# Expert stage of a transformer layer: gather and weight load of one block queued side by side, five blocks ahead

## The reference, cut to what matters

```python
# channel mixing: hierarchical MoE
h = modulate(rmsnorm(x, norm2_g[l]), sh2, sc2)
x = x + g2 * hierarchical_moe(h, ...)
return rmsnorm(x, final_g)

def hierarchical_moe(h, ...):      # 2048 tokens of 1024 per core, 32 experts, 2 per token
    ...                            # top-1 group of 4, then top-2 experts of its 8; combine = gates
    for e in range(N_EXPERTS):
        a, u = jnp.split(t @ w_up[e], 2, axis=-1)             # 1024 -> 2 x 256
        y = y + combine[:, e:e + 1] * ((jax.nn.silu(a) * u) @ w_down[e])
```

## Time and profile before

| | us |
|---|---|
| median of three runs | 1277.55 (1265.26 to 1277.86) |
| the profiled execution | 1271.89 |
| its span, slowest core (core 0) | 1270.2; the eight cores 1251.4 to 1270.2 |
| mean granted TensorE clock, core 0 | 0.811 |
| TensorE busy | 905.8 (71%) |
| VectorE busy | 584.3 (46%) |
| ScalarE busy | 411.5 (32%) |
| GpSimd busy | 333.0 (26%) |

### The profile page before, as it was taken

How to read it: one execution, slowest core, us unless ns; L and a number is a source line. 1 busy time by engine, 2 the same in 40 slices (tenths; PEclk the granted TensorE clock), 3 DMA queues, 4 the chain that set the end, 5 groups by cost and what they waited for, 6 DMA issues and landing times. The chain is left out here.

```text
span 1270.2 us, 17508 instructions; the slowest of 8 cores (1251.4 to 1270.2 us)
## 1 busy us (share of the span) xinstructions
PE 905.8 (71%) x6394; PEld 546.5 (43%) x6394; DVE 584.3 (46%) x1000; ACT 411.5 (32%) x833; POOL 333.0 (26%) x347
## 2 busy tenths in 40 slices
PE   1436999977899999789933357687688788787500
PEld 0134644444544444444422226465465565565300
DVE  1258527341247274424646863333334333343398
ACT  0046321255522212682232202233233333232332
POOL 3100000135300001460000013455456455464200
PEclk9755999975599999889975558788789888898855
DMA  8974154599627434612995106957767668764284
GB/s 173 169 167 131 25 77 66 64 154 151 157 66 108 71 63 69 99 31 104 140 171 144 59 6 133 186 124 148 145 131 140 152 133 177 159 120 104 97 283 173
DMA packets 75010, 154.64 MB, mean 122 GB/s; under 512 B 16930, under 2 KB 53282, under 8 KB 70448
## 3 DMA queue, kind: packets, MB, share of 16 engines
q0 software_dynamic: 61248, 111.28, 50.9%
q1 hardware_dynamic: 13680, 42.25, 9.8%
HBM read 287.20 MB, written 37.22 MB: 255 GB/s over the span
## 5 line engine op out<-in xcount | busy, mean ns | idle before, releaser
L279 PE MATMUL ps<-s_HT,s_ER 128*128 128x512 bf16 (+1 forms) x1232 | 257.0, 358 | 10.1 <-DMA s_ER<-win 4.0
L279 PEld LDWEIGHTS ps<-s_HT,s_ER 128*128 128x128 bf16 x1232 | 111.6, 98 | 142.0 <-issue 15.4
L1085 ACT ACTIVATE s_OV<-ps 128x512 bf16<-128x512 f32 x188 | 101.5, 601 | 143.7 <-PE ps L279 143.5
L1069 DVE TENSOR_TENSOR s_MT<-ps,s_MT 128x256 bf16<-128x256 f32 x94 | 39.9, 425 | 226.1 <-ACT s_MT L1068 151.5
L1039 POOL DMA_INDIRECT s_XG<-hd,s_toki x94 | 105.1, 1119 | 145.3 <-DVE s_MT L998 116.9
L279 PE MATMUL ps<-s_ER,s_MT 128*128 128x512 bf16 x464 | 120.1, 419 | 0.5 <-DVE s_ER L1074 0.5
L1052 PE MATMUL ps<-s_identb,s_XG 128*128 128x128 bf16 x752 | 63.1, 249 | 74.0 <-DMA s_XG<-hd,s_toki 74.0
L1092 POOL DMA_INDIRECT yd<-s_OV,s_rowi x94 | 95.0, 1011 | 61.1 <-ACT s_OV L1085 27.6
L279 PE MATMUL ps<-s_ER,s_XR 64*128 64x256 bf16 (+1 forms) x376 | 71.5, 377 | 51.9 <-DVE s_XR L300 18.6
L279 PE MATMUL ps<-s_MT,s_ER 128*128 128x256 bf16 x832 | 95.5, 273 | 11.2 <-DVE s_MT L1055 10.2
L255 POOL DMA_DIRECT2D s_ER<-win x20 | 17.5, 877 | 292.5 <-PE ps L279 279.4
(11 more groups left out here) (181 smaller groups left out, 1114.8 us busy)
## 6 DMA issues: line engine op xcount, KB each, us to landing
s_ER<-wex POOLq DMA_DIRECT2D x26, 1536.0 KB
s_HT<-wex POOLq DMA_DIRECT2D x21, 1536.0 KB
s_ER<-win POOLq DMA_DIRECT2D x19, 1024.0 KB, 11.2
s_XR<-x SPq DMA_DIRECT2D x32, 512.0 KB, 8.3
s_XR<-wada POOLq DMA_DIRECT2D x8, 1024.0 KB, 14.3
s_HT<-yd SPq DMA_DIRECT2D x16, 512.0 KB, 4.5
out<-s_XR SPq DMA_DIRECT2D x16, 512.0 KB, 3.2
s_ER<-wada POOLq DMA_DIRECT2D x4, 1024.0 KB, 30.7
```

Source lines behind the costliest of these rows:

```text
L279: ins = e.matmul(o, lhsT=l, rhs=r, start=s0, stop=s1)
L1069: S.op("dve", lambda e, b=b, j=j, i=i: e.tensor_tensor(out=acT[i % 2][:, j, :], in0=ps[b][:, 256:512], in1=sab[j], op=ALU.mult), reads=[(" ...
L1085: S.op("act", lambda e, b=b, h=h, yb=yb: e.activation(out=yb[:, h * 512:(h + 1) * 512], in_=ps[b][:], func=AF.Copy), reads=[("ps", b)], wr ...
```

## The change

Four things change.

1. Gathers run further ahead. `XG` gets a fourth pair of buffers (in `ER`, zeroed by one GpSimd memset), `G(0)` to `G(3)` are issued before the loop, `G(4)` in its first iteration, and iteration i issues `G(i + 5)`.
2. In each iteration GpSimd now issues the scatter `O(i-1)`, then `G(i + 5)`, then `W(i + 5)`. The ring of weights has six slots, no longer seven. `YB` has four pairs of buffers, no longer two.
3. The norm has six `xh` buffers, in the room of the seventh ring slot.
4. Only `W(0)` to `W(2)` are issued before the norm's loop; `W(3)` to `W(5)` wait for its last store (`hd`, tile 15).

```diff
-NRING = 7
+NRING = 6
...
-        xh = [OV[:, i * 512:(i + 1) * 512].bitcast(BF16) for i in range(2)]
+        xh = [ER[:, 18432 + i * 1024:18432 + (i + 1) * 1024] for i in range(6)]
...
-        ring = [HTf[:, i * 6144:(i + 1) * 6144] for i in range(3)] + [ER[:, i * 6144:(i + 1) * 6144] for i in range(4)]
+        ring = [HTf[:, i * 6144:(i + 1) * 6144] for i in range(3)] + [ER[:, i * 6144:(i + 1) * 6144] for i in range(3)]
...
-        def W(i):
+        def W(i, after=[]):
...
-                gdma(ring[s], wex_d[n], [], [("wr", s)], ("wr", s))
+                gdma(ring[s], wex_d[n], after, [("wr", s)], ("wr", s))
...
-        for i in range(6):
+        for i in range(3):
             W(i)
...
-            xb = xh[t % 2]
+            xb = xh[t % 6]
...
         n2_lgadd(*pend)
+        for i in range(3, NRING):
+            W(i, [("hd", 15)])
...
+        S.alias([("XG", 3, 0), ("XG", 3, 1)] + [("YB", i) for i in range(4, 8)], ["OB"] + [("OBV", k_, a_) for k_ in range(2) for a_ in range(2)] + [("oh", i) for i in range(6)])
+        S.op("pool", lambda e: e.memset(ER[:, 18432:20480], 0.0), writes=[("XG", 3, 0), ("XG", 3, 1)])
...
-        YB = [OV[:, 2560 + i * 512:2560 + (i + 1) * 512].bitcast(BF16) for i in range(4)]
+        YB = [OV[:, 2560 + i * 512:2560 + (i + 1) * 512].bitcast(BF16) for i in range(4)] + [ER[:, 20480 + i * 1024:20480 + (i + 1) * 1024] for i in range(4)]
+        XGb = [XG[:, i, :] for i in range(6)] + [ER[:, 18432 + i * 1024:18432 + (i + 1) * 1024] for i in range(2)]
...
-                    out=XG[:, (i % 3) * 2 + s, :], out_offset=None, in_=hd_d,
+                    out=XGb[(i % 4) * 2 + s], out_offset=None, in_=hd_d,
...
-                yb = YB[(i % 2) * 2 + s]
+                yb = YB[(i % 4) * 2 + s]
...
-        G(0); W(6); G(1)
+        for i in range(4):
+            G(i)
         T(0)
         for i in range(NI + 1):
-            if i + 2 < NI:
-                G(i + 2)
             if i < NI:
                 U(i)
                 F(i)
...
             if i >= 1:
                 Dn(i - 1)
-                if i - 1 + NRING < NI:
-                    W(i - 1 + NRING)
                 O(i - 1)
+            if i == 0:
+                G(4)
+            if i + 5 < NI:
+                G(i + 5)
+            if i >= 1 and i - 1 + NRING < NI:
+                W(i - 1 + NRING)
```

More of the change, by code:

```diff
@@ L798, in build_program @@
                 ["tmpA", "tmpB", "tmpC", "rd0", "rd1", "qraw", ("qraw", 0), ("qraw", 1)] + [("P", 0, i, hh) for i in range(6) for hh in range(2)])
-        S.alias([("xh", 0), ("xh", 1), ("hTt", 0)], ["ngt", "junk"])
+        S.alias([("hTt", 0), "FGa"], ["ngt", "junk"])
         expand(a2T[:, :], A2b, ["a2T"], "A2b")
@@ L811, in build_program @@
                                                                       for nbk in range(ci * 4, ci * 4 + 4) for hh in range(2)]
-        S.alias([("wr", i) for i in range(3, 7)] + ["OB", "OBV"] + [("oh", i) for i in range(6)], er_old)
+        S.alias([("wr", i) for i in range(3, 6)] + [("xh", i) for i in range(6)], er_old)
         items = [("s", e_) for e_ in range(8)]
@@ L860, in n2_apply @@
             S.op("dve", lambda e: e.tensor_tensor(out=xb, in0=t1f, in1=B2b, op=ALU.add),
-                 reads=["t1f", ("B2b", 0), ("B2b", 1)], writes=[("xh", t % 2)])
-            sdma(hd_d[t * 128:(t + 1) * 128, :], xb, [("xh", t % 2)], [("hd", t)], ("hd", t % 4))
+                 reads=["t1f", ("B2b", 0), ("B2b", 1)], writes=[("xh", t % 6)])
+            sdma(hd_d[t * 128:(t + 1) * 128, :], xb, [("xh", t % 6)], [("hd", t)], ("hd", t % 6))
             bk = nb()
@@ L870, in fn @@
                 return ins
-            S.op("pe", fn, reads=[("xh", t % 2), "identb"], writes=[("ps", bk)])
+            S.op("pe", fn, reads=[("xh", t % 6), "identb"], writes=[("ps", bk)])
             S.op("act", lambda e: e.activation(out=hTt[t % 2], in_=psb.rearrange("p (k n) -> p k n", n=128), func=AF.Copy),
@@ L966, in build_program @@
         slot3 = ER[:, 3 * 6144:4 * 6144]
+        S.alias(["OB"] + [("OBV", k_, a_) for k_ in range(2) for a_ in range(2)] + [("oh", i) for i in range(6)], [("xh", i) for i in range(6)])
         OB = slot3[:, 0:1504].rearrange("p (i n) -> p i n", n=NBLK)
@@ L976, in build_program @@
                                                        in1=tcst.unsqueeze(2).to_broadcast([128, 16, NBLK]), op=ALU.mult), ["OB", "rc"], [("OBV", k_, 1)])
-        S.alias([("OBV", k_, a_) for k_ in range(2) for a_ in range(2)], [])
         bT = nb()
@@ L1013, in build_program @@
         gates()
-        S.alias([("wr", 6)], ["OB"] + [("OBV", k_, a_) for k_ in range(2) for a_ in range(2)] + [("oh", i) for i in range(6)] + [("wr", 6)])
+        S.alias([("XG", 3, 0), ("XG", 3, 1)] + [("YB", i) for i in range(4, 8)], ["OB"] + [("OBV", k_, a_) for k_ in range(2) for a_ in range(2)] + [("oh", i) for i in range(6)])
+        S.op("pool", lambda e: e.memset(ER[:, 18432:20480], 0.0), writes=[("XG", 3, 0), ("XG", 3, 1)])
         G2f = OV[:, 1536:2560]
@@ L1027, in build_program @@
         S.alias([("XT", i, s) for i in range(2) for s in range(2)] + [("acT", i, j) for i in range(2) for j in range(2)] + [("sab", i) for i in range(2)], rt_all)
-        YB = [OV[:, 2560 + i * 512:2560 + (i + 1) * 512].bitcast(BF16) for i in range(4)]
+        YB = [OV[:, 2560 + i * 512:2560 + (i + 1) * 512].bitcast(BF16) for i in range(4)] + [ER[:, 20480 + i * 1024:20480 + (i + 1) * 1024] for i in range(4)]
+        XGb = [XG[:, i, :] for i in range(6)] + [ER[:, 18432 + i * 1024:18432 + (i + 1) * 1024] for i in range(2)]
         S.alias([("YB", i) for i in range(4)], [("B2b", 0), ("B2b", 1), "tb", "ab", "e0"])
         FGt = OV[:, 0:1024]
-        S.alias(["FGa"], [("xh", 0), ("xh", 1)])
         sdma(FGt, fg_d.partition_broadcast(128), [], ["FGa"], "c13")
@@ L1039, in G @@
                 S.op("pool", lambda e, i=i, s=s, c_=c_: e.indirect_dma_start(
-                    out=XG[:, (i % 3) * 2 + s, :], out_offset=None, in_=hd_d,
+                    out=XGb[(i % 4) * 2 + s], out_offset=None, in_=hd_d,
                     in_offset=bass.IndirectOffsetOnAxis(ap=toki[:, s, c_:c_ + 1], axis=0),
                     bounds_check=L - 1, oob_is_err=False),
-                    reads=hdk + ["toki"], writes=[("XG", i % 3, s)], dma=("XG", i % 3, s))
+                    reads=hdk + ["toki"], writes=[("XG", i % 4, s)], dma=("XG", i % 4, s))
         def T(i):
@@ L1051, in fn @@
                     for k in range(8):
-                        ins = e.transpose(psb[:, k * 128:(k + 1) * 128], XG[:, (i % 3) * 2 + s, k * 128:(k + 1) * 128], identb[:])
+                        ins = e.transpose(psb[:, k * 128:(k + 1) * 128], XGb[(i % 4) * 2 + s][:, k * 128:(k + 1) * 128], identb[:])
                     return ins
-                S.op("pe", fn, reads=[("XG", i % 3, s), "identb"], writes=[("ps", s)])
+                S.op("pe", fn, reads=[("XG", i % 4, s), "identb"], writes=[("ps", s)])
                 S.op("dve", lambda e, i=i, s=s, psb=psb: e.tensor_copy(out=XT[i % 2][:, :, s * 128:(s + 1) * 128],
@@ L1085, in Dn @@
                     S.op("act", lambda e, b=b, h=h, yb=yb: e.activation(out=yb[:, h * 512:(h + 1) * 512], in_=ps[b][:], func=AF.Copy),
-                         reads=[("ps", b)], writes=[("YBh", (i % 2) * 2 + s, h)])
+                         reads=[("ps", b)], writes=[("YBh", (i % 4) * 2 + s, h)])
         def O(i):
@@ L1090, in O @@
             for s in range(2):
-                q = (i % 2) * 2 + s
+                q = (i % 4) * 2 + s
                 S.op("pool", lambda e, s=s, q=q, c_=c_: e.indirect_dma_start(
@@ L1095, in O @@
                     reads=[("YBh", q, 0), ("YBh", q, 1), "rowi"], writes=[("yd", i, s)], dma=("YB", q))
-        S.alias([("YBh", q, h) for q in range(4) for h in range(2)], [("YB", q) for q in range(4)])
+        S.alias([("YBh", q, h) for q in range(8) for h in range(2)], [("YB", q) for q in range(8)])
         S.alias([("wrf", r) for r in range(NRING)], [])
-        G(0); W(6); G(1)
+        for i in range(4):
+            G(i)
         T(0)
         for i in range(NI + 1):
-            if i + 2 < NI:
-                G(i + 2)
             if i < NI:
```

## The result

The changed kernel's ratio to the kernel before is 0.9616, 95% interval 0.9545 to 0.9688: faster by 3.8%, about half of the forecast. The executions compared took 1221.83, 1225.05 and 1226.63 us; the median of the first four, 1251.47 us, contains three in which cores of one die ran longer still, and such executions are left out of every ratio here (two of the experiments' profiles, of the gathers issued at U's start and of the rows a step ahead, are of such ones). The one of 1225.05 us was profiled. It lies 44 us above the forecast and 9 us above the end of the range.

A forecast was written before the change was run, and what follows sets the result against it. Gather stalls and the low clock behind them (93 us) were taken to bound the expert loop. Loop gain 68 us (434 to 366) plus norm 22.7 made 91, so 1271.9 us became 1181, range 1152 to 1216.

The forecast's parts named there:

- TensorE allows 344 us, the transfers 362: Expert loop: two limits, with 4 us added for mutual interference, giving a loop of 366 us instead of 434.
- 45 steps at 7.12 us: Expert loop: if all gathers land in time, the steps after the first take 45 x 7.12 = 320.4 us.
- half of the stalls back as waits for weights: Rival, expert loop: half of 93 us stays as weight waits; loop 388 us, total 1203 us; chance 0.2.
- the 1.6 named: Expert loop: sign that the forecast is wrong, GpSimd's gather going over 1.6 us on the mean.
- Norm: Norm stage: six store buffers and three later loads remove VectorE's whole 22.7 us wait for stores to `hd`.
- Loads 3 to 5 hidden: Between norm and loop: `W(3)` to `W(5)`, issued after the last store near 689, cost nothing, hidden under routing.
- Memset: GpSimd zeroing the fourth gather pair: 1.8 us for 2048 columns, cost taken as 0, at most 1.8.
- Gathers in time: Expert loop: gathers issued two blocks earlier; the transposes' wait for `s_XG` falls from 74.0 us to under 15.
- Weights late, 10 to 30 us of waits: Up projection: waits for weight loads of 10 to 30 us appear, most within the loop's first 100 us.
- The 343 us worked out by the Trainium skill: Expert loop's transfers: at the skill page's 8.8 us a load, 27 loads take 19 us less, 343 us.
- the 9.5 us a load of the rows: Weight loads: measured time of one load, 57/6 = 9.5 us, chosen over the skill page's 8.8.
- Clock above 0.93, DMA share 0.8: Expert loop: signs the forecast is right, mean clock rising above 0.93 from 0.88, DMA share to 0.8 from 0.67.

The follow-up runs named there:

- The first four experiments: Norm part alone, against the kernel before (0.9829); against the changed kernel: norm stage of before (0.9829), gathers issued at U's start (0.9721), gate factor behind the copies (0.947).
- the next four: Four of six against the changed kernel, which four not said: transposes ahead (0.9212), no weight loads, no gathers, plain stores, one gather, one gather and one scatter.
- the last two: The other two of those six, not said which; times given: no weight loads 1235.07 us, no gathers 1159.75, plain stores 1213.97, one gather 1177.1.

## Why the prediction was wrong

**The step that failed is the sum: "TensorE allows 344 us, the transfers 362", so 366 for the slowest core.** It knew two limits, both the same for all cores. The slowest core took 413 us, by a limit that stands in neither: U waits for copies behind held signals, 79.0 us in place of 21.5 on the core that I had read, and at a granted clock of 0.93 instead of 0.98 TensorE is busy for 322 us instead of core 4's 300. In the terms of the sum it is the step: 45 steps at 7.12 us were foretold, and the 45 behind the first take 8.58 us on the mean on core 1, 7.13 on core 6. The 66 us between 45 x 8.58 and 45 x 7.12 are nearly all that core 1's loop lies above 344. No rival had it. The one that comes nearest in the time, half of the stalls back as waits for weights (1203 us), is not what happened: core 1 waits for no load. GpSimd's issues were indeed at the root of the loss, but GpSimd was not the bound: its gather took 1.069 us on the mean, far from the 1.6 named, and it stood idle for 158 us waiting for evicted rows (ACT, L1088).

It could have been suspected. The profile page is that of the slowest core, and the earlier trace rows are of core 0. On core 7 of the kernel before the same view reads:

```profile
PE ps L1052 <- DMA s_XG<-hd,s_toki: 47.9, 19, 5.2
PE ps L279 <- DVE s_MT L1055: 39.3, 26, 2.7
PE ps L1052 <- issue: 10.4, 6, 4.2
```

Core 0 has 21.5 us for the copies there, core 3 13.9. Holds in the kernel before: 65 to 130 on cores 4 to 7, at most 13 on the others. All cores had loops of 425 to 434 us all the same: where signals came late, the gathers had longer to land, as I read it. Two waits stood side by side, and taking one away left the other, which grew besides: the activations were late by 3 to 14 us on cores 4 to 7 there, by 23 to 52 on cores 0 to 3 now, and the wait for copies went from core 7's 39.3 us to 54 to 81. What made it grow no run here shows.

**Point by point.** *Norm*: right, 22.7 us foretold, 22.6 measured in the idle time of L860. *Loads 3 to 5 hidden*: right, issued at 685.82 (foretold 689), loop from 736. *Memset*: 1.80 us, as worked out, at no cost. *Gathers in time*: right, 74.0 to 2.7 us. *Weights late, 10 to 30 us of waits*: wrong; none on core 1, 1.8 us on core 6, 9.3 at most (core 4). The undisturbed loops take 343 to 359 us, and without any load 342 to 343, so TensorE's 344 stands and the transfers' 362 was too large, by 3 us at least on the slowest of these cores and by 19 on core 6; with the gate factor behind the copies an undisturbed core moves the same loads in a loop of 334.8. The 343 us worked out by the Trainium skill (HBM Reference, Specifications) came nearer here than the 9.5 us a load of the rows, and that loop undercuts it by 8. *Clock above 0.93, DMA share 0.8*: 0.97 to 0.99 and 0.88 to 0.91 on cores 4 to 7, but 0.93 and 0.77 on core 1. Had the kernel ended with its cores 4 to 7, it would have taken some 1171 us, 10 below the forecast.

**What stays open**: why an indirect transfer's issue holds signals of other engines, and why on one die alone. On the cores with holds some signal records are missing as well (1008 to 1016 of 1023 of TensorE's on cores 0 to 3 of the changed kernel, all there on cores 4 to 7), so the recording itself may have a part; no run here tells that apart. By the Trainium skill (NOTIFIC — the notification-queue block, Overflow: three behaviours, one of which stalls the engine) the recording block's inner pipeline pushes back rather than lose a record, and so can slow an engine; no run here shows it.

## What to carry to other kernels

A hand-over between engines may take microseconds longer on some cores than on others (2.18 us in the step shown), so a loop should not need its last product's signal before the next step's first matmul can start: emit the transposes and copies of the next tile a step ahead, which brought 4% here, more than the rework of the gathers alone. Before costing a change, read the waits of a core of each die, not of the slowest alone; two waits that cover each other show there. Where GpSimd issues indirect transfers, count them per step: three instead of four (with rows left out) brought the loops of all cores within 17 us of each other.

## What the runs showed of the hardware

In each of the twelve profiles the holds lie on the cores of one die, 0 to 3 or 4 to 7, and the other die has none or a few. The first four experiments, on one chip, have them on 0 to 3; the next four, on another chip, and the last two, on a third, on 4 to 7. The kernel before has them on 4 to 7 and the changed kernel on 0 to 3; on which chips these two were profiled is not on record, so that the die is a trait of the chip is not shown. In the changed kernel a hold ended, in the median, 2.05 and 1.99 us after the start of the last gather's issue on cores 1 and 3 and some 1.8 and 1.7 us after it on 0 and 2.
